# A streaming-encoder layer: the first expert table comes in laid out feature by feature, and its blocks are no longer turned on TensorE

## The reference, cut to what matters

```
q = (xb @ w_pq).reshape(T, PEER_HEADS, 2, D_HALF)
s = jnp.einsum('thcd,ckd->thck', q, sub_keys)          # scores of 2 x 128 sub-keys
... top 16 of each half, top 16 of their 256 sums      # eidx: which experts, best: their scores
g = jax.nn.softmax(best, axis=-1)
u = jnp.take(u_tab, eidx, axis=0)                      # first table, 16384 x 2048
a = jax.nn.gelu(jnp.einsum('thkd,td->thk', u, xb))
vv = jnp.take(v_tab, eidx, axis=0)                     # second table, 16384 x 2048
return jnp.einsum('thk,thkd->td', g * a, vv)
```

## Time and profile before

| | |
|---|---|
| median of three executions | 2546.19 us |
| the profiled execution | 2546.42 us |
| its span, first to last instruction | 2544.8 us |
| mean granted PE clock | 0.993 of full |
| busy: PE, DVE, POOL, ACT | 96%, 72%, 42%, 37% of the span |
| DMA | 722.77 MB, mean 284 GB/s |
| first table, first to last matmul | 816.6 to 1786.0 us |
| second table, first matmul | 1792.35 us |

### The profile page before, as it was taken

One profiled execution on the slowest core, in us unless ns is written; L12 is line 12 of the kernel. 1 busy time (PEld: TensorE's weight loads), 2 busy tenths in 40 slices (PEclk: granted clock), 3 DMA queues, 4 the chain that ended last, 5 costly groups with the idle time before them and its releaser, 6 DMA issues.

```text
span 2544.8 us, 41887 instructions
## 1 busy us (share of the span) xinstructions
PE 2444.6 (96%) x15891; PEld 2192.4 (86%) x15891; DVE 1833.0 (72%) x2370; ACT 943.6 (37%) x1158; POOL 1061.8 (42%) x618
## 2 busy tenths in 40 slices
PE   7989999999999999899999999999899999999998
PEld 5878777778999999899999999999787777777777
DVE  3555544554477876788877777776688898888988
ACT  5354543533333333233333333333333334333332
POOL 1020100120006777722577777871344444445441
PEclk9999999999999999999999999999999999999999
DMA  5453544486335666898999999996999999999996
GB/s 192 126 190 117 172 136 142 141 336 238 126 114 144 150 166 179 283 357 333 333 347 344 335 343 338 342 341 249 352 413 411 413 412 412 412 410 412 411 411 280
DMA packets 221525, 722.77 MB, mean 284 GB/s; under 512 B 55672, under 2 KB 105624, under 8 KB 154871
## 3 DMA queue, kind: packets, MB, share of 16 engines
q1 hardware_dynamic: 132304, 397.46, 42.8%
q0 software_dynamic: 87408, 318.89, 35.2%
q10 hardware_dynamic: 1719, 5.26, 0.6%
HBM read 679.70 MB, written 41.83 MB: 284 GB/s over the span
## 4 chain that ended last, share of the span: by engine, by line
PE 60%; DMA 19%; DVE 13%; issue 4%; ACT 1%; SPq 1%; POOL 1%; DVEq 1%; ACTq 0%
PE banks L1329 16%; PE banks L1331 16%; PE banks L1330 16%; DMA a_tile<-a_dense 9%; PE banks L1585 8%; DMA raw<-in_v_tab 5%; DVE h L1282 5%; DVE v_lo L1290 2%; DMA v_raw<-in_v_tab 1%; DMA raw<-in_w_out 1%; DVE ring_lo L1290 1%; DVE ring_lo L860 1%; DVEq L838 1%; DMA a_dense<-gelu_out 1%; POOL g_dense L491 1%
## 5 line engine op out<-in xcount | busy, mean ns | idle before, releaser
L1329 PE MATMUL banks<-xT_hi,ring_hi 128*128 128x256 f32 (+1 forms) x2304 | 686.1, 298 | 11.7 <-DVE gelu_out L1227 10.1
L1331 PE MATMUL banks<-xT_hi,ring_lo 128*128 128x256 f32 (+1 forms) x2304 | 664.0, 288 | 0.0
L1330 PE MATMUL banks<-xT_lo,ring_hi 128*128 128x256 f32 (+1 forms) x2304 | 663.5, 288 | 0.0
L491 POOL DMA_INDIRECT g_dense<-route,route_place x256 | 462.2, 1806 | 306.3 <-DVE route_place L1194 184.6
L528 POOL DMA_INDIRECT v_row<-in_v_tab,route_place x128 | 339.0, 2648 | 428.0 <-DVE h L1282 374.6
L781 ACT ACTIVATE ring_hi<-banks 128x1024 fp32r<-128x1024 f32 x256 | 262.5, 1026 | 625.3 <-PE banks L1585 585.8
L1236 DVE TENSOR_TENSOR ring_lo<-banks,ring_hi 128x1024 fp32r<-128x1024 f32 x256 | 313.1, 1223 | 217.1 <-ACT ring_hi L781 178.4
L1329 PEld LDWEIGHTS banks<-xT_hi,ring_hi 128*128 128x128 f32 x2304 | 439.1, 191 | 13.1 <-DVE ring_lo L1236 12.6
L1330 PEld LDWEIGHTS banks<-xT_lo,ring_hi 128*128 128x128 f32 x2304 | 439.5, 191 | 0.0
L1331 PEld LDWEIGHTS banks<-xT_hi,ring_lo 128*128 128x128 f32 x2304 | 438.8, 190 | 0.0
L860 DVE TENSOR_TENSOR ring_lo<-raw,ring_hi 128x2048 fp32r<-128x2048 f32 x72 | 165.0, 2291 | 219.9 <-ACT ring_hi L556 219.5
(11 more groups left out here) (248 smaller groups left out, 4012.8 us busy)
## 6 DMA issues: line engine op xcount, KB each, us to landing
raw<-in_u_tab SPq DMA_DIRECT2D x128, 1024.0 KB
v_raw<-in_v_tab SPq DMA_DIRECT2D x64, 1024.0 KB, 15.1
raw<-in_v_tab SPq DMA_DIRECT2D x64, 1024.0 KB
raw<-in_w_in SPq DMA_DIRECT2D x160, 256.0 KB, 3.4
raw<-in_w_out SPq DMA_DIRECT2D x64, 256.0 KB, 4.8
g_dense<-zeros POOLq DMA_DIRECT2D x16, 1024.0 KB, 28.6
raw<-in_w_pq SPq DMA_DIRECT2D x64, 256.0 KB, 3.6
a_dense<-gelu_out SPq DMA_DIRECT2D x128, 128.0 KB
```

The source lines that it names most:

```text
L491: pool.indirect_dma_start(out=places, out_offset=bass.IndirectOffsetOnAxis(ap=routeU[:, t, 2, j:j + 1], axis=0), in_=route[:, t, 0, j:j + ...
L1329: MM(out, h1, h2, start=first, stop=False)
L1330: MM(out, h1, l2, start=False, stop=False)
L1331: return MM(out, l1, h2, start=False, stop=last)
```

## The change

The host hands in a second copy of the first table, `u_turned`: its block m is the 128 experts m, m + 128, ... with the features on the partitions, which is what the matmul wants as its stationary operand. The row gathers still use `u_tab`.

- PE no longer turns blocks; lines 1585 and 1606 and their waits go. A result goes to bank m % 4.
- ACT makes one high part of 128x2048 from SBUF (`u_hi`), DVE one low part of 128x2048 with both inputs in SBUF (`u_lo`), which overwrites the raw block.
- High parts, raw blocks and results are rings of four. SP loads block m when PE is through with block m - 4.
- `scaled(m - 3)` stands behind the dots of block m; `gelu(m - 4)` behind `u_hi(m)`, and ACT issues the store itself. PE waits at the end for the scaling, not for the gelu.
- Low parts 0 and 1 are made before the first table starts, amid the last weight block's work.
- The raw slots of the second table and two of the buffers for its gathered rows trade places with those of the first.

```diff
-        rawu = [raw[:, 0, :], raw[:, 1, :], at("raw2", MX + 24, [P, D])[:, :], at("raw3", MX + 32, [P, D])[:, :]]
+        rawu = [at("u_raw0", MX + 24, [P, D])[:, :], at("u_raw1", MX + 32, [P, D])[:, :], raw[:, 0, :], raw[:, 1, :]]
+        uH = [ringH[:, 0, :], ringL[:, 0, :], ringH[:, 1, :], ringL[:, 1, :]]
+        uL = [at(f"u_lo{i}", kb, [P, D], F32R)[:, :] for i, kb in enumerate((MX + 24, MX + 32, 80, 88))]
...
             def u_load(m, slot):
-                sp.dma_start(rawu[slot], u_v[:, ds(m, 1), :].rearrange("p o d -> p (o d)")).then_inc(u_in[slot], 16)
+                sp.dma_start(rawu[slot], I["u_turned"][ds(m, 1), :, :].rearrange("o p d -> p (o d)")).then_inc(u_in[slot], 16)
...
-            with sp.Fori(2, P // UR) as it:
+            with sp.Fori(1, P // UR) as it:
                 for q in range(UR):
-                    u_next(it * UR + q, q)
-                    store_gelu(it * UR + (q - 6), q % 2)
+                    sp.wait_ge(u_used, it * UR + (q + 1 - UR))
+                    u_load(it * UR + q, q)
...
+            def u_hi(m):
+                act.wait_ge(u_in[m % UR], 16 * (m // UR) + 16)
+                if m >= UR:
+                    act.wait_ge(u_used, m - UR + 1)
+                else:
+                    act.wait_ge(split_used, BASE_U + 1 + m // 2)
+                A(uH[m % UR], rawu[m % UR], ACT.Copy).then_inc(u_hi_done, 1)
...
             def gelu(m, k):
-                act.wait_ge(u_scaled, m + 3)
+                act.wait_ge(u_scaled, m + (UR + 1))
                 A(aout[:, k, :], aout[:, k, :], ACT.Gelu_apprx_tanh).then_inc(gelu_done, 1)
+                act.wait_ge(gelu_done, m + 1)
+                act.dma_start(Ad[m], aout[:, k, :]).then_inc(a_store[k], 16)
...
+            def u_lo(m):
+                dve.wait_ge(u_hi_done, m + 1)
+                V.tensor_tensor(uL[m % UR], rawu[m % UR], uH[m % UR].bitcast(F32), ALU.subtract).then_inc(u_lo_done, 1)
...
             for m in range(P):
-                u_lo(m, m % 2)
+                if m >= 2:
+                    u_lo(m)
...
                 while dots < dots_after(m):
                     dot(dots)
                     dots += 1
-            scaled(P - 2, 0)
-            scaled(P - 1, 1)
+                if m >= UR - 1:
+                    scaled(m - (UR - 1))
...
-            def u_step(m, it, q, turns=True):
+            def u_step(m, q):
                 pe.wait_ge(u_scaled, m + 1)
+                pe.wait_ge(u_lo_done, m + 1)
                 for b in range(KC):
-                    if turns and b in (2, 8):
-                        u_turns(m + 1, it + (q + 1) // UR, (q + 1) % UR, b // 8)
-                    if b % 8 == 0:
-                        pe.wait_ge(u_lo_done, m * 2 + (b // 8 + 1))
                     c = slice(b * P, (b + 1) * P)
-                    k = q % 2
-                    last = three(bank[k][:, 0:TU], ringH[:, k, c], ringL[:, k, c], xTh[:, b, 0:TU], xTl[:, b, 0:TU], b == 0, b == KC - 1)
+                    last = three(bank[q][:, 0:TU], uH[q][:, c], uL[q][:, c], xTh[:, b, 0:TU], xTl[:, b, 0:TU], b == 0, b == KC - 1)
                 last.then_inc(u_used, 1)
...
-            pe.wait_ge(gelu_done, P + 2)
+            pe.wait_ge(u_scaled, P + UR)
...
+    rows = arrays["in_u_tab"][0].reshape(P, P, KC, P)
+    arrays["in_u_turned"] = _np.ascontiguousarray(rows.transpose(1, 3, 2, 0)).reshape(P, P, D)
```

More of the change, by code:

```diff
@@ L386, in _ @@
             v_weights(1, 1)
-            for m in range(P - 6, P - 2):
-                store_gelu(m, m % 2)
+            for k in range(2):
+                sp.wait_ge(a_store[k], 16 * 2)
             sp.wait_ge(dot_done, DOTS)
@@ L768, in _ @@
                         A(bv[:, 2 * quarter:2 * quarter + 2, :], bv[:, 2 * quarter:2 * quarter + 2, :], ACT.Exp).then_inc(best_exp, 1)
+            for m in range(2):
+                u_hi(m)
             def best_weights(n, heads):
@@ L773, in best_weights @@
                 A(bv[:, heads, :], bv[:, heads, :], ACT.Exp).then_inc(best_exp, 1)
[L775 to L781, removed]
             def gelu(m, k):
-                act.wait_ge(u_scaled, m + 3)
+                act.wait_ge(u_scaled, m + (UR + 1))
                 A(aout[:, k, :], aout[:, k, :], ACT.Gelu_apprx_tanh).then_inc(gelu_done, 1)
+                act.wait_ge(gelu_done, m + 1)
+                act.dma_start(Ad[m], aout[:, k, :]).then_inc(a_store[k], 16)
             q_evac(3)
             score_evac(3)
[L790 to L796, removed]
+            for m in range(1, P):
+                if m >= 2:
+                    u_hi(m)
                 for quarter, part in QUARTER_IN_U.get(m - 1, ()):
@@ L801, in _ @@
                     best_weights(QUARTERS + (NT - 1 - tile_part(m - 1)[0]), slice(0, PH))
-                if m:
-                    gelu(m - 1, (m - 1) % 2)
-            gelu(P - 1, 1)
+                if m >= UR:
+                    gelu(m - UR, m % 2)
             def v_hi(m, s, sets):
@@ L815, in w_hi @@
                 A(wth[:, par, :, :], wt[:, par, :, :], ACT.Copy).then_inc(wh_done, 1)
+            act.wait_ge(u_used, P - 3)
             v_hi(0, 0, 0)
+            gelu(P - 4, 0)
+            act.wait_ge(dot_done, DOTS)
+            A(adot[:, :], adot[:, :], ACT.Gelu_apprx_tanh).then_inc(dot_gelu, 1)
+            gelu(P - 3, 1)
+            gelu(P - 2, 0)
+            act.wait_ge(u_used, P - 1)
+            v_hi(1, 1, 0)
             w_hi(0, 0)
-            v_hi(1, 1, 0)
+            gelu(P - 1, 1)
             v_hi(2, 2, 0)
@@ L1214, in _, with scaled @@
                     drain()
-                for n in SWEEPS_AT.get(s, ()):
+                for i, n in enumerate(SWEEPS_AT.get(s, ())):
                     sweep(n)
+                    if s == 15:
+                        u_lo(i)
                 for quarter, part in QUARTER_IN_PQ.get(s, ()):
                     routing_quarter(quarter, part)
-            def scaled(m, k):
+            def scaled(m):
                 dve.wait_ge(u_used, m + 1)
                 if m >= 2:
-                    dve.wait_ge(a_store[k], 16 * (m // 2))
+                    dve.wait_ge(a_store[m % 2], 16 * (m // 2))
                 if m == 0:
                     dve.wait_ge(root_ev, 1)
[L1227 to L1237, removed]
+                V.tensor_tensor(aout[:, m % 2, :], bank[m % UR][:, 0:TU], rootB[:, :], ALU.mult).then_inc(u_scaled, 1)
             def dot(i):
@@ L1288, in _ @@
             for m in range(P):
-                dve.wait_ge(hi_done, BASE_V + m + 1)
-                V.tensor_tensor(vL[m % VS], vraw[m % VS], vH[m % VS].bitcast(F32), ALU.subtract).then_inc(lo_done, 1)
+                if m:
+                    v_lo(m)
                 if m + 2 < P:
```

59 lines of the change are left out of this document (19 added, 40 removed).

## The result

The changed kernel took 2553.69 us (median of 16, 2548.08 to 2567.63), the kernel before 2545.22 us in the same sessions (median of 16, 2541.85 to 2550.2). The ratio is 1.0037 with a 95% interval of 1.0024 to 1.005: slower by 9 us. Forecast were 2575 us, slower by 28. The direction was right, and so was what holds POOL; the size was three times too large.

The account below looks back on a forecast made before the run. PE was taken to bound the long stage at 7.48 us a block, POOL close behind. The terms +26, +9.5, -13, +21, -10.5 and -5 sum to +28 on 2546.4 us: 2575 us, range 2526 to 2614.

Parts of the forecast that it names:

- What bounds the kernel: Long stage: PE sets 7.48 us a block, 5.76 without turns; POOL is free for only 0.45 us a block.
- What holds POOL: New low part, both inputs in SBUF, holds POOL instructions starting within it, as dots do at 1.10 us each.
- rival A: Whole kernel: the new low part doesn't hold POOL; -56 us, 2490 us, chance 0.12.
- Term (1): Up to the first row gather: 27 low parts hold POOL, +29.7, less up to 3.8 regained; +26 us.
- quarter 1: Before the first row gather: this quarter is routed earlier, which takes up to 3.8 of POOL's 4.13 us wait.
- Term (2): Placements with gathers, 1007.9 to 1083.5 us: POOL paces 8.6 blocks, each 1.10 us longer; +9.5 us.
- Term (4): Long stage: 65.75 low parts hold POOL 0.77 us each, 50.6 us, less 29.4 that are free; +21 us.
- (3): Row gathers alone, 1083.5 to 1225.5 us: DMA's bound is 126.7 us, 129 taken; -13 us.
- (5): The end, 9.5 blocks in 68.5 us without placements: PE needs 54.7, 58 taken; -10.5 us.
- (6): Hand-over to the second table: of PE's 6.30 us idle about 1.5 us stay; -5 us.
- rival C: Whole kernel: holds and gains cancel at 0.65 us a low part; +4 us, 2550 us, chance 0.08.

Follow-up runs that it names:

- half_before: The kernel before the change with every second placement of tile 1 left out (64 of the long stage's 128): 2545.41 us, ratio 0.9994.
- half_after: The changed kernel with every second placement of tile 1 left out (64 of the long stage's 128): 2458.2 us, ratio 0.9660.
- psum_all: The changed kernel with ACT also copying the raw block into PSUM from block 2 on, as the low part's first input: 2502.24 us, ratio 0.9826.

## Why the prediction was right in kind and wrong in size

**What bounds the kernel.** Right: POOL was free for only 0.45 us a block, and PE's 1.7 us couldn't be had beyond that. `half_before` and `half_after` show both sides.

**What holds POOL.** Right, and the main thing to get right. The rule of the Trainium skill ("SBUF — State Buffer", Who interferes with whom), by which such a subtraction doesn't stop the making of descriptors, agrees with the direct DMAs of this trace (0.89 us within it and outside), but not with the indirect ones: 3.63 us against 1.55, and rival A with it is out. The prediction took the rule to cover gathers too, but rightly went by the earlier trace rows. Rival A was wrong in its number too, since `psum_all` shows the dots alone keeping the long stage at 494 us.

**Term (1), +26 forecast, +13.5 measured with the earlier start: the step that failed.** The low parts' hold was priced well: of 27 low parts, 25 held a POOL instruction, for 31.4 us (29.7 forecast). What is given back against it was not: the forecast had 3.8 us for quarter 1, the list got back 6.8 and 8.8. The 6.8 are holds of the routing's own DVE instructions (comparisons, products and sums, also with two SBUF inputs). They held POOL 9.5 us before and 2.7 now, as four of the five long ones follow a low part at once. The 8.8 are POOL's waits, 23.5 us before and 14.7 now beyond the usual 0.30. Three of them before (placements 61, 81 and 97), then those of the changed kernel (33, 61, 81 and 97):

```profile
902.92 1.55 POOL L491 DMA_INDIRECT g_dense<-route,route_place  x1 [4.82 <-issue]
947.99 1.55 POOL L491 DMA_INDIRECT g_dense<-route,route_place  x1 [4.14 <-DMA g_dense<-route,route_place]
986.00 1.55 POOL L491 DMA_INDIRECT g_dense<-route,route_place  x1 [4.81 <-DMA g_dense<-route,route_place]
```

```profile
848.44 2.32 POOL L477 DMA_INDIRECT g_dense<-route,route_place  x1 [3.03 <-DMA g_dense<-route,route_place]
915.20 1.55 POOL L477 DMA_INDIRECT g_dense<-route,route_place  x1 [2.31 <-issue]
972.56 1.55 POOL L477 DMA_INDIRECT g_dense<-route,route_place  x1 [3.13 <-DMA g_dense<-route,route_place]
1004.17 1.55 POOL L477 DMA_INDIRECT g_dense<-route,route_place  x1 [2.19 <-DMA g_dense<-route,route_place]
```

Quarter 1 gave 1.1 us and not 3.8, since placement 33 (4.13 us before) now waits 3.03 us for landings. The 2.41 us ahead of the first gather stand in the same group and went unused; 2.1 of them are gone. The gap ahead of placement 61 fell by 2.5; the kernel waits for no semaphore there, and what it is stays open. The waits for landings at placements 81 and 97 fell by 1.0 and 2.6, and one at placement 49 grew by 0.6; why wasn't tried. With all holds, 12.8 us before and 37.5 now, the sum is 24.7 - 8.8 = +15.9, that of the table; the 2.4 us of an earlier start make the rest. The second profiles give the same +15.9, and `psum_all`, free of the low parts' hold, passes (1) in 222.7 us, 8.4 under before.

**Term (2), +9.5 forecast, +2.7 measured.** The 8 low parts held POOL for 7 us, but the dots' hold fell from 12 us to 8 and 10.6: a dot right behind a low part finds POOL in step. I used that argument in (4) and not here. That it is the reason is argued and not shown.

**Term (4), +21 forecast, +24.8 measured.** The two profiles have 43 and 54 us more hold than before, 0.65 and 0.82 for each of 66 low parts; 0.77 was taken. (The low parts' own hold is 60 us, the dots' fell from 92 to 77 and 87.) The waits for landings, put at nothing, grew by 6.3 and 4.6 us.

**Terms (3), (5), (6)** held: -12.5 for -13, and -17.7 for -15.5 together; PE idles 1.16 us ahead of the second table, 6.30 before. The rest of the program, priced at nothing, ended 3.8 us shorter; that wasn't tried by itself.

The terms that failed are (1) by 12.5 and (2) by 6.8 us; the rest by 3.8, (5, 6) by 2.2 and, the other way, (4) by 3.8 and (3) by 0.5: 21, the 28 forecast less the 7 found. What (1) and (2) have in common: one price of the hold was multiplied out, and what neighbouring holds take from each other was left out. And in (1) the prediction had POOL free for the 4.13 us at quarter 1 alone, and took its waits for landings as unchanged. The first gather, at 1020.9 us, lay below the 1025 to 1045 that were named as a sign. The total lies at rival C's, but not for C's reason, since a low part did cost the forecast's 0.65 to 0.82 us in the long stage and more before it.

## What to carry to other kernels

An engine that is busy throughout a stage hides the next one: before work is taken off it, ask for the slack of each queue in that stage, gaps and waits for landings counted, and what the new form of the work does to it. When a list is going to run slower, look through all its waits, the short ones, those for landings and those marked as issue too: here 8.8 us of them came back as a gain, and only 3.2 of these were waits for a neighbour. And an order that was tuned to one pace (gathers from placement 104) has to be moved with the pace: here that number alone turned slower into faster.

## What the runs showed of the hardware that was not expected

- A DVE subtraction or dot with both inputs in SBUF holds back an indirect DMA instruction of POOL that starts within it: a held placement ended 1.42 to 1.47 us after the low part that held it (68 cases). The low part is not prolonged to speak of (2.28 us in the median, 2.34 at most). A direct DMA instruction that starts within such a subtraction takes its usual 0.89 us (43 cases). The same subtraction with one input in PSUM holds nothing (1.55 us within 2.28). Copying an operand into free PSUM banks for this alone, 1.9 us of ACT a block, bought 54 us in the same session.
- Holds of neighbouring instructions don't add. Dots held POOL for 78 to 88 us of the long stage with low parts between them and for 103 without.
- A full 32-bit product of 128x128 by 128 columns cost PE 0.22 us ((9.3 - 5.76) / 16), a transpose of the same size 0.11 (1.74 / 16).
